# Value rows of a gated unit in alternation over two token blocks, and a later place for the first spatial product

## The reference, cut to what matters

```python
def chunked_sgu_mixer(h, w_in, ln_w, ln_b, w_s, b_s, w_out):
    z = h @ w_in                                   # 512 x 1024 @ 1024 x 6144
    u, v, g = jnp.split(z, 3, axis=-1)
    u = jax.nn.gelu(u)
    v = layer_norm(jax.nn.gelu(v), ln_w, ln_b)     # over the 2048 channels of v
    v = v.reshape(B, S // CHUNK, CHUNK, A_GROUPS, A_GROUP_DIM)
    w_causal = w_s * causal[None]
    s = jnp.einsum('gts,bnsgc->bntgc', w_causal, v) + b_s.T[None, None, :, :, None]
    y = u * s.reshape(B, S, A_WIDTH) * jax.nn.silu(g)
    return y @ w_out                               # 2048 -> 1024
```

## Time and profile before

| | us |
|---|---|
| median of three runs (lowest to highest) | 1441.17 (1438.26 to 1447.72) |
| the profiled execution, its own time | 1438.62 |
| its span in the profile | 1436.9 |
| TensorE busy | 1300.3 (90%) |
| VectorE busy | 866.6 (60%) |
| ScalarE busy | 587.7 (41%) |
| value rows, first ScalarE copy to last statistics | 813.5 to 895.1 |
| pairs of the first half, first unit to last spatial product | 880.9 to 985.2 |

### The profile page before, as it was taken

The page is one execution under the profiler, slowest core; times in us unless marked ns, Lnnn a source line. Parts: engine busy times, 40 slices in busy tenths (PEclk is TensorE's granted clock), DMA queues, the critical chain, the costliest instruction groups (busy, mean ns, idle before and its releaser), DMA issues.

```text
span 1436.9 us, 17824 instructions
## 1 busy us (share of the span) xinstructions
PE 1300.3 (90%) x6005; PEld 1045.3 (73%) x6005; DVE 866.6 (60%) x1249; ACT 587.7 (41%) x830; POOL 189.0 (13%) x191
## 2 busy tenths in 40 slices
PE   5887557799889999999999998999999989999697
PEld 2666446688778878788888876888788867767576
DVE  4746996565666533245445596665366556777763
ACT  3455612255234422134333355443233336557532
POOL 5025944200000000000000000110011002224100
PEclk9899878899989999999999999999999989999899
DMA  8552211141454533333332232323233322322131
GB/s 294 159 156 59 58 44 45 30 131 61 147 138 140 163 95 93 89 89 99 100 90 88 59 117 59 88 88 106 85 88 88 94 75 81 92 69 72 48 99 59
DMA packets 204432, 137.80 MB, mean 96 GB/s; under 512 B 7074, under 2 KB 191569, under 8 KB 204384
## 3 DMA queue, kind: packets, MB, share of 16 engines
q1 hardware_dynamic: 200784, 134.40, 31.7%
q0 software_dynamic: 1376, 1.73, 0.4%
q10 hardware_dynamic: 2224, 1.05, 0.3%
HBM read 135.06 MB, written 2.10 MB: 95 GB/s over the span
## 4 chain that ended last, share of the span: by engine, by line
PE 67%; DVE 18%; ACT 6%; issue 5%; DMA 2%; POOL 1%; DVEq 0%; ACTq 0%; SPq 0%; POOLq 0%
PE banks L384 20%; PE banks L385 19%; PE banks L386 19%; DVE w_lo L368 3%; DMA raw<-in_ada_w 2%; ACT w_hi L356 1%; DVE score L1711 1%; PE banks L686 1%; DVE m L1708 1%; DVE xc L2144 1%; PE banks L1025 1%; DVE vt L2055 1%; DVE t_s L2164 1%; DVE e L2053 1%; ACT e L1468 1%
## 5 line engine op out<-in xcount | busy, mean ns | idle before, releaser
L368 DVE TENSOR_TENSOR w_lo<-raw,w_hi 128x1024 fp32r<-128x1024 f32 x204 | 264.1, 1302 | 210.2 <-ACT w_hi L356 207.5
L384 PE MATMUL banks<-h_hi,w_hi 128*128 128x512 f32 x824 | 334.3, 406 | 18.3 <-issue 4.7
L385 PE MATMUL banks<-h_lo,w_hi 128*128 128x512 f32 x824 | 325.9, 395 | 0.0
L386 PE MATMUL banks<-h_hi,w_lo 128*128 128x512 f32 x824 | 325.8, 395 | 0.0
L356 ACT ACTIVATE w_hi<-raw 128x1024 fp32r<-128x1024 f32 x204 | 213.0, 1051 | 178.4 <-PE banks L386 158.0
L384 PEld LDWEIGHTS banks<-h_hi,w_hi 128*128 128x128 f32 x824 | 158.2, 192 | 61.5 <-issue 13.8
L385 PEld LDWEIGHTS banks<-h_lo,w_hi 128*128 128x128 f32 x824 | 158.4, 192 | 34.3 <-issue 2.4
L386 PEld LDWEIGHTS banks<-h_hi,w_lo 128*128 128x128 f32 x824 | 157.7, 191 | 34.0
L384 PE MATMUL banks<-n_hi,w_hi 128*128 128x512 f32 x256 | 102.8, 402 | 1.2 <-DVE xT L1913 1.2
L384 PE MATMUL banks<-hid_hi,w_hi 128*128 128x512 f32 x256 | 102.0, 399 | 0.0
L385 PE MATMUL banks<-hid_lo,w_hi 128*128 128x512 f32 x256 | 101.9, 398 | 0.0
(11 more groups left out here) (368 smaller groups left out, 2044.3 us busy)
## 6 DMA issues: line engine op xcount, KB each, us to landing
raw<-in_mlp_w SPq DMA_DIRECT2D x64, 512.0 KB, 4.0
raw<-in_a_w_in SPq DMA_DIRECT2D x48, 512.0 KB, 3.8
raw<-in_ada_w SPq DMA_DIRECT2D x40, 512.0 KB, 4.8
raw<-in_w_in SPq DMA_DIRECT2D x28, 512.0 KB, 3.8
raw<-in_b_w_in SPq DMA_DIRECT2D x24, 512.0 KB, 4.0
raw<-in_a_w_out SPq DMA_DIRECT2D x16, 512.0 KB, 4.0
raw<-in_b_w_out SPq DMA_DIRECT2D x16, 384.0 KB, 3.5
raw<-in_w_out SPq DMA_DIRECT2D x8, 512.0 KB, 4.1
```

The source lines that it names most:

```text
L368: dve.tensor_tensor(dst, src, hi, ALU.subtract).then_inc(split_lo, 1)
L384: pe.matmul(dst, l_hi, r_hi, start=first, stop=False)
L385: pe.matmul(dst, l_hi, r_lo, start=False, stop=False)
L386: return pe.matmul(dst, l_lo, r_hi, start=False, stop=last)
```

## The change

Two things are moved; no instruction is added or taken away.

1. In the loop over the token blocks the second part of a block's work is put one step later. ScalarE issues the copy and the square of block `t`, then the tanh of block `t - 1`. VectorE issues the inside of the tanh of block `t`, then gelu and statistics of block `t - 1`.
2. TensorE's order in a turn becomes u0, g0, u1, mix 0, g1, mix 1. The wait on `evac` (banks 0 to 3 read out) is split: u1 needs bank 0 (count 13), g1 and mix 1 need banks 1 and 2 (count 15); before, u1 waited for all four (count 16).

```diff
@@ TensorE
-                    for cc in range(2):
-
-                        pe.wait_ge(h_ready, H_Y + 8 * half + cc - 1 + 2 * i)
-                        if cc == 1:
-                            pe.wait_ge(evac, E_V + 16)
-                        for s in range(2):
...
+                    pe.wait_ge(h_ready, H_Y + 8 * half - 1 + 2 * i)
+                    half_unit(0, 0)
+                    half_unit(0, 1)
+                    pe.wait_ge(h_ready, H_Y + 8 * half + 2 * i)
+                    pe.wait_ge(evac, E_V + 13)
+                    half_unit(1, 0)
+                    mix(0)
+                    pe.wait_ge(evac, E_V + 15)
+                    half_unit(1, 1)
+                    mix(1)
@@ ScalarE
-                for t in range(TT):
+                for t in range(TT + 1):
                     n, bank = 4 * g + t, 4 * (1 - g % 2) + t
...
+                    if t < TT:
+                        act.activation(vt[:, t, 512 * g:512 * (g + 1)], banks[:, bank, :], ACT.Copy, scale=rs[:, t:t + 1])\
+                           .then_inc(v_copied, 1)
+                        act.wait_ge(v_stat, V0 + n - 1)
+                        act.activation(e0[:, t % 2, :], banks[:, bank, :], ACT.Square, scale=rs[:, t:t + 1]).then_inc(evac, 1)
+                    if t:
+                        act.wait_ge(v_inner, n)
+                        act.activation(e0[:, (t - 1) % 2, :], e0[:, (t - 1) % 2, :], ACT.Tanh).then_inc(v_tanh, 1)
@@ VectorE
+                for t in range(TT + 1):
+                    if t < TT:
+                        n = 4 * g + t
...
+                        dve.tensor_scalar(e, e, GELU_C * GELU_A, GELU_C, ALU.mult, ALU.add).then_inc(v_aff, 1)
+                        dve.wait_ge(v_aff, n + 1)
+                        dve.tensor_tensor(e, e, v, ALU.mult).then_inc(v_inner, 1)
+                    if t:
+                        n = 4 * g + t - 1
...
+                        dve.wait_ge(v_tanh, n + 1)
+                        dve.scalar_tensor_tensor(v, e, 1.0, v, ALU.add, ALU.mult).then_inc(v_gelu, 1)
+                        dve.wait_ge(v_gelu, n + 1)
+                        dve.bn_stats(vst[:, t - 1, g, :], v).then_inc(v_stat, 1)
```

More of the change, by code:

```diff
@@ L1009, in _, with half_unit, mix @@
                 with pe.Fori(0, 4) as i:
-                    for cc in range(2):
-                        pe.wait_ge(h_ready, H_Y + 8 * half + cc - 1 + 2 * i)
-                        if cc == 1:
-                            pe.wait_ge(evac, E_V + 16)
-                        for s in range(2):
[L1016 to L1022, removed]
+                    def half_unit(cc, s):
+                        u = U_UG + 24 * half + 2 * cc + s
+                        pe.wait_ge(split_lo, u + 1 + RING * i)
+                        for k in range(KT):
+                            last = three(pe, banks[:, 4 * (1 - cc) + s, :], unit(w_hi, u, P)[:, k, :],
+                                         unit(w_lo, u, P)[:, k, :], n_hi[:, k, :], n_lo[:, k, :],
+                                         k == 0, k == KT - 1)
+                        last.then_inc(w_used, 1)
+                    def mix(cc):
                         pe.wait_ge(vh_made, 8 * half + cc + 1 + 2 * i)
@@ L2045, in _ @@
                     v_norms(V_NORMS[g])
[L2046 to L2057, removed]
+                for t in range(TT + 1):
+                    if t < TT:
+                        n = 4 * g + t
+                        e, v = e0[:, t % 2, :], vt[:, t, 512 * g:512 * (g + 1)]
+                        dve.wait_ge(evac, E_V + n + 1)
+                        dve.wait_ge(v_copied, n + 1)
+                        dve.tensor_scalar(e, e, GELU_C * GELU_A, GELU_C, ALU.mult, ALU.add).then_inc(v_aff, 1)
[3 more added lines that the diff above has]
+                        n = 4 * g + t - 1
+                        e, v = e0[:, (t - 1) % 2, :], vt[:, t - 1, 512 * g:512 * (g + 1)]
+                        dve.wait_ge(v_tanh, n + 1)
+                        dve.scalar_tensor_tensor(v, e, 1.0, v, ALU.add, ALU.mult).then_inc(v_gelu, 1)
+                        dve.wait_ge(v_gelu, n + 1)
+                        dve.bn_stats(vst[:, t - 1, g, :], v).then_inc(v_stat, 1)
             dve.wait_ge(v_stat, V0 + 16)
```

## The result

| | before | changed |
| --- | --- | --- |
| median of 12 runs each on the same chip | 1441.11 us | 1447.57 us |
| range | 1438.26 to 1447.72 | 1444.71 to 1454.42 |
| profiled execution | 1438.62 us | 1447.05 us |
| its span | 1436.9 us | 1445.3 us |

The ratio is 1.0042 with the interval [1.0026, 1.0058], or about 6.1 us. That lies within one per cent, as forecast.

A forecast was written before the change was run, and what follows sets the result against it. TensorE, busy 90% of the span, was taken as the bound. Terms -2.7 - 1.35 + 6.6 + 3.3 = +5.85 us on the profiled 1438.62 us gave 1444.5 us, range 1437.5 to 1449.

The forecast's parts named there:

- split waits in the value stage: TensorE's waits for ring splits behind groups 1 and 2 of the value rows go: -2.7 us, bounds -1.2 to -2.7.
- mix 1 of the first turn: First turn: TensorE's 5.75 us wait becomes 4.4 us, one product later, so mix 1 starts 2.9 us earlier.
- slow clock behind its wait: First turn, behind the wait at mix 1: TensorE's slow clock charged at 1.55 us, leaving net -1.35 us.
- end wait with its clock, half 0: End of the first half: TensorE waits 3.3 us for `h_lo` at step 7, plus 1.65 us of slow clock.
- Part 1: Loop over the token blocks: steady block 3.25 us (3.17 before), last statistics 1.3 us earlier in each group.
- The first turn: TensorE's first turn: no wait at mix 0, a 4.4 us wait at mix 1, net -1.35 us with slow clock.
- slow stretch behind mix 1, so I charge 1.55: First turn: the slow clock seen before ahead of mix 1 now falls behind it, costing 1.55 us.
- The later turns: Other seven turns: `vh` of pair 1 comes 1.2 us or more before mix 1 needs it; cost 0.
- Rival C: `vh` of pair 1 late in every turn; at 2 us over, 14 us more, 1458 us; chance 0.03.
- The ends: End of each half: last body ends at M + 15.45, step 7 comes at M + 12.13; 3.3 us wait each, +6.6.
- Rival A: End of each half: the two engines' body absorbs the later start, no wait at the last step; 1434.6 us; chance 0.12.
- The clock behind them: Slow TensorE clock behind the two end waits: 1.65 us each, +3.3 us, range 0.2 to 3.3.

The follow-up runs named there:

- e1: Changed loop over the token blocks, with TensorE's order and single wait on `evac` from the kernel before: 1439.52 us, ratio 0.9975.
- e2: Kernel before with its old loop over the token blocks, but TensorE's new order in the turns: 1450.78 us, ratio 1.0065.
- e3: Changed kernel, but u1 precedes mix 0 only in the first turn of half 0, other seven turns in the old order: 1438.17 us, ratio 0.9967.
- e5: Changed kernel, but the last turn of each half has the old order, mix 0 ahead of u1: 1443.47 us, ratio 1.0003.
- e6: Changed kernel plus 12 matmuls with unused result ahead of step 7 of each half's first output tile: 1445.38 us, ratio 1.0026.
- e9: Changed kernel with ScalarE's second split in a pair's body moved ahead of the tanh: 1441.01 us, ratio 0.9987.
- e7: Changed kernel, but VectorE makes `vh` of both pairs ahead of pair 0's body in each turn: 1441.37 us, ratio 0.9991.
- e8: e4 with `vh` of pair 1 made right behind `vh` of pair 0, TensorE in the old order: 1435.86 us, ratio 0.9948.
- e4: e1, but the square waits for the gelu of the block whose buffer it takes, not for its statistics: 1435.39 us, ratio 0.9956.

## Why the prediction was right, step by step

| term | predicted | measured | where |
| --- | --- | --- | --- |
| split waits in the value stage | -2.7 | -2.78 | lead at 880.85 |
| mix 1 of the first turn | -2.9 | -2.96 | from -2.78 to -5.74 |
| slow clock behind its wait | +1.55 | +2.47 | from -5.74 to -3.27 |
| end wait with its clock, half 0 | +4.95 | +4.84 | from -3.27 to +1.57 |
| the same, half 1 | +4.95 | +4.94 | from +1.56 to +6.50 |
| sum | +5.85 | +6.50 | |

**Part 1** held in its working too: blocks 3.25 us apart, as laid out, and the last statistics 12.05 us behind the first copy, where 12.07 was counted. e1 shows that the gain is the loop's own.

**The first turn** held in where the wait goes (4.30 us at mix 1 for 4.4 predicted). The term "slow stretch behind mix 1, so I charge 1.55" is the one that was mis-sized: it measured 2.47. The 1.55 us were taken from the stretch behind mix 0 before. The windows show what differs, first the kernel before, where mix 0 starts at 897.96:

```profile
894.00:895.00 1.00, 0.00 (x0) 0.00 (x0) 0.97 (x2) 0.98 (x1) 0.00 (x0) 0.63 0.00 0
...
901.00:902.00 1.00, 1.00 (x5) 0.77 (x5) 0.08 (x1) 1.00 (x2) 0.00 (x0) 0.95 0.75 216
```

and the changed kernel, where mix 1 starts at 907.85:

```profile
906.00:907.00 1.00, 0.00 (x0) 0.00 (x0) 0.93 (x3) 1.00 (x2) 0.00 (x0) 0.58 0.00 0
...
912.00:913.00 1.00, 1.00 (x4) 0.81 (x3) 1.00 (x2) 0.07 (x1) 0.00 (x0) 0.50 0.20 60
913.00:914.00 1.00, 1.00 (x5) 0.79 (x5) 1.00 (x3) 0.00 (x0) 0.00 (x0) 1.00 0.00 0
```

Before, the clock is low from 894.3 to 901.1, and 3.7 us of that pass inside the wait, where nothing is lost. In the changed kernel it is low from 906.2 to 913.0, for as long, but only 1.7 us of that lie in the shorter wait. So 5.1 us of work instead of 3.1 run at half rate, and half of that time is lost. In e1, where the wait of 4.39 us stands at mix 0 (898.64), the clock falls only at 899.0:

```profile
898.00:899.00 1.00, 0.35 (x3) 0.36 (x4) 0.49 (x2) 0.99 (x2) 0.00 (x0) 1.00 0.00 0
...
902.00:903.00 1.00, 1.00 (x5) 0.81 (x4) 0.00 (x0) 1.00 (x2) 0.00 (x0) 0.79 0.95 268
```

It is back at 902.4, so 3.4 us of work are slow and 1.7 us are lost. The same reading holds for the other waits at mix 1: 5.0 to 5.8 us of slow work and 2.4 to 2.8 us lost in e2, e3, e5 and e6, 3.1 us and 1.56 in e9. The cost is half of the part of the slow stretch that falls into work, and it does not grow with the wait. What sets the moment at which the clock falls stays open.

**The later turns** held: M + 4.20 for `vh` against 4.1 to 5.2 predicted, and no wait at mix 1 (982.87 without one). Rival C is out.

**The ends** carried the sign and came out as worked: M + 15.40 against M + 12.17, with 15.45 and 12.13 predicted. e2 has the same wait with the loop unchanged, e3 has none with the later turns in the old order: so the late order of the later turns is its cause, not the loop. Rival A, that the body would absorb the delay, fails: the body gave back little more than the wait for GpSimd that had been counted (15.40 instead of 15.45). **The clock behind them** (1.65 each, from 3.64 us idle) was right in size, and e6 shows that the idle time is its cause: with the array busy, 1.4 and 1.5 us go away.

I took the clock as certain in the sum, where the Trainium skill (TensorE: Matmul & The Clock Gate, "What's actually happening") lets the point of change differ from run to run. For this length of wait the traces agree with the firm charge: behind 3.12 to 3.17 us it fell all four times, in two kernels. At shorter waits the outcome does vary: in e7 it fell behind 2.33 us and not behind 2.38.

The median came out at 1447.57 and not 1444.5. Of the 3.1 us, 2.5 are the distance between the median before and its profiled execution, which the text had named, and about 0.6 is the sum's own error (0.65 in the trace): the mis-sized term, 0.92 too small, less small ones of the other sign.

## What to carry to other kernels

Moving a product later gives slack to the input it waits for, and takes the same time from everything behind its output. In the middle of a loop later work may pay that; at the loop's end nothing does, so follow the chain to the first consumer outside the loop and set its arrival against the time it is wanted, in every turn and not only where the wait was seen. When a wait turns out to move rather than go, shorten the chain instead: release a buffer at its last reader, and don't queue a covered job ahead of the next link. Count the clock behind a new idle stretch as a term of its own.

## What the runs showed of the hardware

What an isolated idle stretch of TensorE costs in clock, in otherwise dense work, by its length:

| idle, us | granted clock behind it, and cost beside the wait |
| --- | --- |
| 1.42, 1.66, 1.70 (e5, e9) | 1.00; 0.3 us |
| 2.02 (e5), 2.33 (e7) | fell to 0.50; about 1.9 us |
| 2.38, 2.46 (e7) | 1.00; 0.3 us |
| 2.92 (e8), 2.93 (e4), both at mix 0 | 1.00; 0.1 us |
| 3.12 to 3.17 (changed kernel, e2) | fell all four times, 1.7 to 1.8 us |
| 3.37 (e9, at mix 1) | fell, 1.56 us |
| 4.25 to 5.75 (all at a spatial product: before, changed kernel, e1, e2, e3, e5, e6) | fell all seven times, 1.55 to 2.8 us |

From 2.0 to 2.9 us the outcome did not follow the length: the two shortest of these waits lost the clock, the four longer ones kept it. From 3.1 us on it fell every time in this table, and so it did in all twelve traces at the wait for a split near 385 us (3.28 to 4.17 us idle). The fall can also come only behind the wait. In e5 the matmuls behind the wait of 2.02 us start at full speed, and slow down about a microsecond later (0.40 to 0.63 us a record):

```profile
989.43 0.40 PE L385 MATMUL banks<-h_lo,w_hi 128*128 128x512 f32 x1
...
990.29 0.63 PE L385 MATMUL banks<-h_lo,w_hi 128*128 128x512 f32 x1
```
